# Token halves of the gate matmuls dealt out anew over the attention units of a two-layer hybrid encoder

## The chip, the cores and the metric

The kernel runs on one core of one Trainium2 chip. The metric is the device time of one execution in microseconds, as the median of several runs; lower is better.

## The reference, cut to what matters

Two layers are computed for 512 prompt tokens and 8 streams of 16 tokens each (640 tokens in all, model width 1024). What matters of a layer:

```
z  = x @ w_in                      # q, k, v of mixer A; latents of mixer B
yA = sliding-window attention, prompt (chunks of 64, window 128) and 8 streams (cache of 128)
yB = latent attention,         prompt (512 keys, causal by chunk) and 8 streams (cache of 512)
g  = sigmoid(x @ w_gate + b_gate)  # 1024 -> 2048, needs x alone
h  = g[:, :1024] * (yA @ w_proj_a) + g[:, 1024:] * (yB @ w_proj_b)
x  = LN1(alpha * x + h @ w_out);  x = LN2(alpha * x + ConvGLU(x))
```

The logits x @ w_gate depend on neither mixer, so their matmuls can stand anywhere between the units of attention.

## The kernel before, in words

Everything is written out by hand: each engine has its own program, in a fixed order, and they meet at semaphores. Dense products split both operands into a high and a low part (`x_hi`, `x_lo`, `w_hi`, `w_lo`) and take three matmuls per tile. A slab of weights arrives by a DMA of SP's queue in `w_raw`; ACT writes its high part (`high`, the copy of L791) and POOL its low part (`low`, the subtraction of L704), half a slab at a time.

Attention is a list of 40 units (`UNITS`), u = 0 to 39: u = 0 to 7 are mixer A's prompt ("Ap", 128 queries and four heads each), u = 8 to 15 mixer A's streams ("As", one stream each), u = 16 to 39 mixer B ("Bp", "Bp", "Bs" in turn). PE's loop over u does, in this order: `scores(u + 2)` (L1782 for Ap, L1792 and L1793 for As, L1798 for Bp, L1805 to L1808 for Bs), `turn(u)` (transposes of the probabilities, L1826), the gates behind u, and `values(u - 1)` (L1859, L1862, L1863, L1869). DVE's loop does `peaks(u + 2)` (bias, maximum, negated maximum: L1237 to L1240 for Ap, L1243 to L1246 for As), its half of the copy of the turned probabilities (L1274, not for Ap), `normalise(u + 1)` (L1262, L1263, L1267), which `turn(u + 1)` waits for, and `take_out(u - 1)` (L1285, L1291). ACT's loop does its part of the turned copy (L872, L873), `exps(u + 2)` (L849 for Ap, L853 for As) and `take_gate` (L881).

A gate here is one token half (320 tokens) of one tile of 128 gate columns: 24 matmuls of L1892 into PSUM bank 7, g = 0 to 31 (`NG`). Gates 0 and 1 stand ahead of the loop; `gates_before(u)` says how many stand before unit u, and PE, ACT and SP's order of stores and loads all follow from it. After a gate with odd g, `take_gate` also calls `high` for half a slab of later gate weights (the slab two further on), and POOL's `low` of the same half follows at once. SP's loop over quarters of gates places `load_gate`, `store_gate` and `load_cache` (the cache of a mixer B stream, three DMAs) by the same function.

Of the kernel before, what the change touches and what calls it, by code (L numbers as in the profile page):

```python
# [133 lines left out]
UNITS = [("Ap", i, g) for i in range(NB) for g in range(GH // 2)] + [("As", r, 0) for r in range(NREQ)]  # L134
# [4 lines left out]
NU = len(UNITS)  # L139
# [5 lines left out]


NG = 4 * KD
assert NU % 4 == 0 and NG == 2 + 3 * NU // 4


def gates_before(u):
    return 2 + 3 * (u // 4) + min(u % 4, 3)


def gate_behind(u):

    return range(gates_before(u), gates_before(u + 1))


def quarter_at_scores(u):  # L160
    return 0 if u < 2 else 4 * gates_before(u - 2)
# [2001 lines left out]
```

## Time and profile before

| | |
|---|---|
| median of 3 runs | 1901.82 us (1900.15 to 1901.82) |
| profiled execution | 1900.86 us |
| its span | 1899.1 us |
| PE busy | 1847.1 us, 97% of the span |
| DVE, ACT, POOL busy | 1014.7, 654.4, 541.0 us |

Mixer A takes some 80 us in each layer (layer 0 from 126 us on, layer 1 from 1056 us on). In a timeline a row gives the start, the duration, the engine, the line and the operation, and in brackets how long the engine was idle ahead of it and who ended that. PE's instructions overlap, so a row's duration reaches into the next. "PEclk" is the granted clock as a share of the full one: 1.00 is 2.4 GHz and 0.50 is 1.2 GHz.

### The profile page before, as it was taken

How to read it: one execution, taken by the hardware profiler on the slowest of the kernel's cores; microseconds unless marked ns; L12 is line 12 of the kernel's file. 1: busy time of each engine (PE TensorE's matmuls, PEld its weight loads, DVE VectorE, ACT ScalarE, POOL GpSimd, SP SyncE). 2: the span in 40 equal slices, each digit the busy share in tenths (PEclk: the TensorE clock that was granted, in tenths of full speed). 3: DMA queues.
4: the chain of work that ended last, by engine and by line, in shares of the span. 5: the costliest groups of instructions: out<-in, count | busy, mean ns of one | idle time of the engine just before them, and what ended most of it. 6: DMA issues, size and time to landing. Idle time of an engine off the chain costs nothing. (4 is left out here: it accounts for less than half of the span.)

```text
span 1899.1 us, 31847 instructions
## 1 busy us (share of the span) xinstructions
PE 1847.1 (97%) x12458; PEld 1755.0 (92%) x12458; DVE 1014.7 (53%) x1597; ACT 654.4 (34%) x1381; POOL 541.0 (28%) x244
## 2 busy tenths in 40 slices
PE   8899999999999999999999999999999999999996
PEld 8877888899999999999998788889999999999995
DVE  3567544558854423443765865445697443234447
ACT  4135333532433212332332443334334332132323
POOL 2321211133143234332422311112322333433331
PEclk9999999999999999999999999999999999999998
DMA  6443233232122122121241613323311211222121
GB/s 183 141 140 82 90 110 99 93 129 83 45 92 80 50 89 89 66 72 56 88 135 56 171 47 126 104 69 132 117 68 67 89 55 67 77 89 81 49 74 56
DMA packets 67875, 171.19 MB, mean 90 GB/s; under 512 B 16360, under 2 KB 34456, under 8 KB 60056
## 3 DMA queue, kind: packets, MB, share of 16 engines
q1 hardware_dynamic: 67768, 169.71, 27.6%
q8 instruction: 74, 1.21, 0.3%
q14 instruction: 33, 0.27, 0.1%
HBM read 150.90 MB, written 19.59 MB: 90 GB/s over the span
## 5 line engine op out<-in xcount | busy, mean ns | idle before, releaser
L704 POOL TENSOR_TENSOR w_lo<-w_raw,w_hi 128x1024 fp32r<-128x1024 f32 (+2 forms) x230 | 530.7, 2316 | 1285.8 <-ACT w_hi L791 1266.6
L791 ACT ACTIVATE w_hi<-w_raw 128x1024 fp32r<-128x1024 f32 (+2 forms) x228 | 218.2, 975 | 463.3 <-PE ps L1625 427.1
L1625 PE MATMUL ps<-x_hi,w_hi 128*128 128x320 f32 x1408 | 322.0, 310 | 4.0 <-POOL w_lo L704 4.0
L1625 PE MATMUL ps<-x_lo,w_hi 128*128 128x320 f32 x1408 | 321.3, 309 | 0.0
L1625 PE MATMUL ps<-x_hi,w_lo 128*128 128x320 f32 x1408 | 321.3, 309 | 0.0
L1625 PEld LDWEIGHTS ps<-x_hi,w_hi 128*128 128x128 f32 x1408 | 236.0, 188 | 4.6 <-issue 4.4
L1625 PEld LDWEIGHTS ps<-x_lo,w_hi 128*128 128x128 f32 x1408 | 235.9, 188 | 0.0
L1625 PEld LDWEIGHTS ps<-x_hi,w_lo 128*128 128x128 f32 x1408 | 235.9, 188 | 0.0
L1525 DVE TENSOR_SCALAR f_conv<-f_ext,vec 128x656 f32<-128x656 f32 x44 | 64.6, 1469 | 202.2 <-ACT tail L1016 199.7
L1892 PE MATMUL ps<-x_hi,w_hi 128*128 128x320 f32 x512 | 164.9, 322 | 0.0
L1892 PE MATMUL ps<-x_lo,w_hi 128*128 128x320 f32 x512 | 159.2, 311 | 0.0
L1892 PE MATMUL ps<-x_hi,w_lo 128*128 128x320 f32 x512 | 159.2, 311 | 0.0
L1625 PE MATMUL ps<-hf_hi,w_hi 128*128 128x320 f32 x624 | 143.0, 310 | 0.0
L1625 PE MATMUL ps<-hf_lo,w_hi 128*128 128x320 f32 x624 | 142.5, 309 | 0.0
L1625 PE MATMUL ps<-hf_hi,w_lo 128*128 128x320 f32 x624 | 142.2, 309 | 0.0
L1540 DVE TENSOR_TENSOR hf_lo<-f_h,hf_hi 128x640 f32 x44 | 83.9, 1908 | 46.7 <-ACT hf_hi L1024 46.7
L1625 PEld LDWEIGHTS ps<-hf_hi,w_hi 128*128 128x128 f32 x624 | 104.7, 188 | 0.3
L1625 PEld LDWEIGHTS ps<-hf_lo,w_hi 128*128 128x128 f32 x624 | 104.7, 188 | 0.0
L1625 PEld LDWEIGHTS ps<-hf_hi,w_lo 128*128 128x128 f32 x624 | 104.6, 188 | 0.0
L1892 PEld LDWEIGHTS ps<-x_hi,w_hi 128*128 128x128 f32 x512 | 97.4, 190 | 1.2 <-ACT logits L881 0.3
L1892 PEld LDWEIGHTS ps<-x_lo,w_hi 128*128 128x128 f32 x512 | 97.5, 190 | 0.0
L1892 PEld LDWEIGHTS ps<-x_hi,w_lo 128*128 128x128 f32 x512 | 97.1, 190 | 0.0
(281 smaller groups left out, 3189.5 us busy)
## 6 DMA issues: line engine op xcount, KB each, us to landing
w_raw<-in_slabs SPq DMA_DIRECT2D x84, 1024.0 KB, 4.9
w_raw<-in_slabs SPq DMA_DIRECT2D x20, 768.0 KB, 4.1
gate_logits<-logits SPq DMA_DIRECT2D x64, 160.0 KB, 1.9
gates<-gate_logits SPq DMA_DIRECT2D x16, 640.0 KB, 6.2
w_raw<-in_slabs SPq DMA_DIRECT2D x16, 640.0 KB, 3.7
ckvc<-in_ckvc SPq DMA_DIRECT2D x16, 256.0 KB, 2.7
ckvc_t<-in_ckvc_t SPq DMA_DIRECT2D x16, 256.0 KB, 3.0
w_raw<-in_slabs SPq DMA_DIRECT2D x6, 512.0 KB, 5.9
```

The source lines that it names most:

```text
L704: pool.tensor_tensor(to, w_raw[:, s % 2, c], hi.bitcast(F32), ALU.subtract).then_inc(wlo_ready, 1)
L791: A(w_hi[:, s % 2, c], w_raw[:, s % 2, c], ACT.Copy).then_inc(whi_ready, 1)
L1525: link(TSC(f_conv[:, 0:NC_], f_ext[:, 2:EXT], w(2), vec[:, bass.ds(V_CB + j, 1)], ALU.mult, ALU.add))
L1540: TT(row(hf_lo, jj), f_h[:], row(hf_hi, jj).bitcast(F32), ALU.subtract).then_inc(fh_lo_ready, 1)
L1625: ins = MM(out_[:, a, :], w, x[:, t, a * HT:(a + 1) * HT], start=t == 0 and w is wh and x is hi, stop=t == tiles - 1 and w is wl)
L1892: ins = MM(ps[:, 7, 0:HT], w, x[:, t, a * HT:(a + 1) * HT], start=t == 0 and w is wh and x is x_hi, stop=t == KD - 1 and w is wl)
```

## The change

The number of gates behind each unit was given by a formula, three in every four units, with none behind u = 3, 7, 11, 15 and so on. Now it is a list. Each of the 8 units of mixer A's prompt has one gate, the streams of mixer A have one behind every second unit (u = 8, 10, 12, 14), and mixer B keeps three in four. The total over mixer A is 12 either way, so that two gates move from behind u = 9 and u = 13 to behind u = 3 and u = 7, and from u = 16 on every gate is where it was.

```diff
 NG = 4 * KD
-assert NU % 4 == 0 and NG == 2 + 3 * NU // 4
+HALVES = [1] * 8 + [1, 0] * 4 + [1, 1, 1, 0] * 6
+assert len(HALVES) == NU and [x[0] for x in UNITS[:16]] == ["Ap"] * 8 + ["As"] * 8 and sum(HALVES) == NG - 2
 
 
 def gates_before(u):
-    return 2 + 3 * (u // 4) + min(u % 4, 3)
+    return 2 + sum(HALVES[:u])
```

Every line behind the list stands one line further down in the kernel of the change (L1892 is L1893 there, and so on).

**PE, end of unit u = 2 to the start of u = 4.** The first rows are of before: values of u = 1, scores of 5, turn of 3, values of 2, scores of 6, turn of 4, and the gate of u = 4.

```order
L1859 MATMUL ps<-probs_t,v_tok 64x256 x2
L1782 MATMUL ps<-k_t,q_a 128x256 x4
L1826 MATMUL ps<-ident,probs 128x128 x8
L1859 MATMUL ps<-probs_t,v_tok 64x256 x4
L1782 MATMUL ps<-k_t,q_a 128x256 x4
L1826 MATMUL ps<-ident,probs 128x128 x8
L1892 MATMUL ps<-x_hi,w_hi 128x320
```

The same place on PE in the change:

```order
L1860 MATMUL ps<-probs_t,v_tok 64x256 x2
L1783 MATMUL ps<-k_t,q_a 128x256 x4
L1827 MATMUL ps<-ident,probs 128x128 x8
L1893 MATMUL ps<-x_hi,w_hi 128x320
L1893 MATMUL ps<-x_lo,w_hi 128x320
L1893 MATMUL ps<-x_hi,w_lo 128x320
```

A gate (these three rows eight times over) now stands between the turn of u = 3 and the values of u = 2; the same happens at u = 7.

**ACT, units 12 and 13 of before.** Each unit is the turned copy (L873), the exponentials (L853, L855) and, where there is a gate, L881; L791 is the high part of weights behind an odd gate, here g = 11.

```order
L873 ACTIVATE probs_t<-ps 128x128
L853 ACTIVATE probs,st_sum<-ps,st_nm 128x144
L855 ACTIVATE st_es<-st_d 128x1
L881 ACTIVATE logits<-ps,vec 128x320
L791 ACTIVATE w_hi<-w_raw 128x1024
L873 ACTIVATE probs_t<-ps 128x128
L853 ACTIVATE probs,st_sum<-ps,st_nm 128x144
L855 ACTIVATE st_es<-st_d 128x1
L881 ACTIVATE logits<-ps,vec 128x320
```

In the change the same gate g = 11 stands behind u = 10, and these are units 10, 11 and 12 on ACT:

```order
L874 ACTIVATE probs_t<-ps 128x128
L854 ACTIVATE probs,st_sum<-ps,st_nm 128x144
L856 ACTIVATE st_es<-st_d 128x1
L882 ACTIVATE logits<-ps,vec 128x320
L792 ACTIVATE w_hi<-w_raw 128x1024
L874 ACTIVATE probs_t<-ps 128x128
L854 ACTIVATE probs,st_sum<-ps,st_nm 128x144
L856 ACTIVATE st_es<-st_d 128x1
L874 ACTIVATE probs_t<-ps 128x128
L854 ACTIVATE probs,st_sum<-ps,st_nm 128x144
L856 ACTIVATE st_es<-st_d 128x1
L882 ACTIVATE logits<-ps,vec 128x320
```

Before, the unit behind the conversion of weights had a gate; in the change the unit behind it (u = 11) has none.

## Rows read from the trace of the kernel before

**Rows 1.** The page: busy time by engine; TensorE's granted clock in 40 slices.

```profile
PE 1847.1 (97%) x12458; PEld 1755.0 (92%) x12458; DVE 1014.7 (53%) x1597; ACT 654.4 (34%) x1381; POOL 541.0 (28%) x244
...
PEclk9999999999999999999999999999999999999998
```

**Rows 2.** Lines, PE, 1071 to 1151 us: busy, mean, idle before.

```profile
L1826 PE MATMUL ps<-ident,probs 128*128 128x128 f32 x69 | 10.9, 284 | 3.1 <-DVE probs L1267 3.1
```

**Rows 3.** PE's timeline behind u=3 and u=7 (layer 1): start, duration, row, idle.

```profile
1092.68 1.09 PE L1826 MATMUL ps<-ident,probs 128*128 128x128 f32 x8 [1.35 <-DVE probs L1267]
...
1114.80 0.44 PE L1826 MATMUL ps<-ident,probs 128*128 128x128 f32 x2 [0.92 <-DVE probs L1267]
```

**Rows 4.** PE's timeline around u=11, layer 1.

```profile
1129.65 0.44 PE L1792 MATMUL ps<-kc_t,q_a 64*64 64x128 f32 x4
...
1130.09 0.44 PE L1826 MATMUL ps<-ident,probs 128*128 128x128 f32 x2
...
1131.16 0.44 PE L1792 MATMUL ps<-kc_t,q_a 64*64 64x128 f32 x4
1131.43 0.25 PE L1793 MATMUL ps<-k_t,q_a 64*64 64x16 f32 x4
1132.14 0.44 PE L1826 MATMUL ps<-ident,probs 128*128 128x128 f32 x2 [0.46 <-DVE probs L1267]
```

**Rows 5.** PE's timeline behind the gate of u=12, layer 1.

```profile
1136.93 0.25 PE L1793 MATMUL ps<-k_t,q_a 64*64 64x16 f32 x4
1137.10 0.44 PE L1826 MATMUL ps<-ident,probs 128*128 128x128 f32 x2
```

**Rows 6.** POOL's timeline: the low parts behind the gates of u=6 and u=12.

```profile
1111.58 2.36 POOL L704 TENSOR_TENSOR w_lo<-w_raw,w_hi 128x1024 fp32r<-128x1024 f32 x1 [9.93 <-ACT w_hi L791]
...
1137.74 2.41 POOL L704 TENSOR_TENSOR w_lo<-w_raw,w_hi 128x1024 fp32r<-128x1024 f32 x1 [9.57 <-ACT w_hi L791]
```

**Rows 7.** DVE's timeline behind the gates of u=6 and u=12.

```profile
1112.14 1.81 DVE L1245 SCALAR_TENSOR_TENSOR st_nm<-st_mx,nsink_s 128x1 f32<-128x1 f32 x1
...
1137.94 2.22 DVE L1245 SCALAR_TENSOR_TENSOR st_nm<-st_mx,nsink_s 128x1 f32<-128x1 f32 x1
...
1140.86 0.30 DVE L1267 TENSOR_SCALAR probs<-probs,st_ri 128x144 f32<-128x144 f32 x1
```

**Rows 8.** PE's timeline at u=15: scores of u=17, turn of 15.

```profile
1146.65 0.71 PE L1798 MATMUL ps<-kb,qb 100*128 100x128 f32 x4
1147.19 0.38 PE L1826 MATMUL ps<-ident,probs 128*128 128x128 f32 x2
```

**Rows 9.** DVE's timeline: the normalising of u=6.

```profile
1102.64 1.14 DVE L1267 TENSOR_SCALAR probs<-probs,st_ri 128x256 f32<-128x256 f32 x4
```

**Rows 10.** PE's timeline: the turn of u=6.

```profile
1105.31 1.09 PE L1826 MATMUL ps<-ident,probs 128*128 128x128 f32 x8
```

**Rows 11.** Stretches: us, PE, PEld, DVE, ACT, POOL, PEclk, DMA, GB/s.

```profile
1087.00:1093.50 6.50, 5.15 (x41) 3.53 (x40) 5.47 (x13) 3.94 (x15) 0.00 (x0) 1.00 0.46 166
...
1147.80:1151.20 3.40, 3.07 (x14) 1.85 (x13) 3.32 (x8) 0.90 (x5) 2.27 (x1) 1.00 0.09 34
1151.20:1154.60 3.40, 3.40 (x15) 3.40 (x14) 1.66 (x7) 1.07 (x3) 0.00 (x0) 0.50 0.00 0
```

**Rows 12.** PE's timeline, around the gate of u=16, both layers.

```profile
220.30 0.44 PE L1826 MATMUL ps<-ident,probs 128*128 128x128 f32 x2 [0.33 <-DVE probs L1267]
...
224.09 0.39 PE L1862 MATMUL ps<-probs_t,vc 128*128 128x128 f32 x2
...
1150.92 0.51 PE L1826 MATMUL ps<-ident,probs 128*128 128x128 f32 x2 [0.33 <-DVE probs L1267]
...
1156.26 0.38 PE L1862 MATMUL ps<-probs_t,vc 128*128 128x128 f32 x2
```

**Rows 13.** SP's timeline: the last DMA of stream 0's cache.

```profile
1141.71 0.63 SPq L623 DMA_DIRECT2D krc_t<-in_krc_t  x1
```

**Rows 14.** The tile ckvc_t in layer 1: DMA issue to landing.

```profile
DMA to landing us min/median/max: 2.6/3.0/6.1
```

## The prediction

> **What bounds the kernel now.** The page comes first: PE is busy for 1847.1 of 1899.1 us, no other engine for much over half the span, and its granted clock stands at 9 tenths or more in nearly every slice [rows 1]. The time is therefore PE's own work plus the moments in which it waits. The change keeps every matmul, so only those moments can move, and only in mixer A. The view by lines, for mixer A of layer 1, puts all of them before the turn of a unit's probabilities: 3.1 us, all released by DVE's normalising, L1267 [rows 2]. PE's timeline then shows the places, and each lies behind a unit without a gate: 1.35 us before turn(4), behind u = 3, and 0.92 us before turn(8), behind u = 7 [rows 3]; 0.46 us before turn(12), behind u = 11 [rows 4]; and 0.33 us before turn(16), behind u = 15 [rows 12]. Layer 0 has the same four waits in the same sizes, the last of them among the rows.
>
> Why they are there follows from the order of the two programs. DVE does peaks(u + 2) before normalise(u + 1), so that turn(u + 1) waits until DVE has worked through the scores that PE issued just ahead of turn(u). A gate gives PE 24 matmuls, and 3.5 us, to do in the meantime. With a gate the margin is comfortable even in the prompt: the last normalising of u = 6 ends at 1102.64 + 1.14 = 1103.78 us [rows 9], and PE begins that turn only at 1105.31 us [rows 10], 1.53 us later.
>
> **What the change removes.** A gate behind u = 3 and behind u = 7 covers both waits, 1.35 + 0.92 = 2.27 us a layer. The units now look like u = 5 and 6 of before, and I take the cover for complete: 3.5 us of gate against 1.35 us. Behind g = 7 and g = 9 POOL's low part of weights now falls among DVE's peaks of stream units that PE follows with a gate; it costs up to 2.3 us of DVE (next part) and is hidden by those 3.5 us. Were that cover gone, each would cost PE about what the wait before turn(8) costs now, 0.92 us.
>
> **What it adds.** The units 9, 11, 13 and 15 have no gate now, 11 and 15 alone had none before. I price each from rows of this kernel with the same neighbours.
>
> (1) u = 9 follows a gate with even g, without a conversion of weights, as u = 11 does before: 0.46 us [rows 4].
>
> (2) u = 11 follows g = 11, an odd gate. Behind it ACT converts half a slab and POOL subtracts, for 2.41 us from 1137.74 us on in the trace [rows 6]. In just these 2.41 us a DVE instruction on a single column, L1245, which starts 0.20 us after POOL's, takes 2.22 us and ends with it. The same instruction took 1.81 us behind the gate of u = 6, where it started at 1112.14 us and POOL's ran from 1111.58 for 2.36 us [rows 6, 7]: in both places it ends 0.01 to 0.02 us after POOL's. So DVE stands until POOL has finished. Before, u = 13 with its gate stood behind this place. In the change nothing does. DVE's chain gives the time of the turn: the normalising ends at 1140.86 + 0.30 = 1141.16, and a turn starts 0.06 us behind it, at 1141.22 (estimate, the 0.06 from the next rows: hence also the choice not to round). PE gets there earlier. Its turn starts at 1137.10 [rows 5]; from a turn to the next scores without a gate between is 1131.16 - 1130.09 = 1.07 us, and those scores end 1131.43 + 0.25 - 1131.16 = 0.52 us after their start [rows 4]. That is 1137.10 + 1.07 + 0.52 = 1138.69, and the wait is 1141.22 - 1138.69 = 2.53 us. The bounds are 0.46 us (POOL disturbs nothing) and 2.53 us; I take 2.53, since the row it comes from has the same instructions in the same order up to the missing gate.
>
> (3) u = 13 follows an even gate, but PE now has the longer scores of u = 16 to do. From scores(13) to turn(12) is 1132.14 - 1129.65 = 2.49 us through DVE [rows 4]. PE needs 1130.09 - 1129.65 = 0.44 us to its turn, 1.07 us to the scores and 0.71 us for them [rows 8], 2.22 us in all. The wait is 0.27 us.
>
> (4) u = 15 follows g = 13 before and after: 0.33 us, unchanged.
>
> **Loads and stores.** Gates 5 to 11 come one or two units earlier, the loads of gate slabs with them. Stream 0's cache is asked for at the end of scores(15) either way, and scores(18) now follow it by one gate and not two. After scores(15) PE has 0.44 + 1.07 + 0.27 + 0.71 us to turn(14), a gate unit of 5.0 us and about 1 us more, some 8 us in all. The cache's last DMA takes 0.63 us to issue [rows 13], and the loads of that tile land in 2.6 to 6.1 us, the longest being the one that before stood behind a slab [rows 14]. That slab now comes two units earlier. I cost this at nothing; without the cover the worst landing would still be in time by about half a microsecond.
>
> **The sum of the waits.** Per layer 1.35 + 0.92 + 0.46 = 2.73 us go, and 0.46 + 2.53 + 0.27 = 3.26 us come: 0.53 us more, 1.06 us over both layers.
>
> **The clock.** One thing beside the waits moves with them. In layer 1 the stretch 1147.8 to 1151.2, with small matmuls, no gate and 0.33 us idle, is followed by 3.4 us at 0.50, which is 1.2 GHz; the stretch around u = 3, with 1.35 us idle but the fuller matmuls of the prompt, keeps 1.00 (2.4 GHz) [rows 11]. The slow stretch costs what the gate of u = 16 shows in the two layers: 1156.26 - 1150.92 = 5.34 us against 224.09 - 220.30 = 3.79 us, 1.55 us [rows 12]. Layer 0 has the same instructions at full clock, so it is partly luck where it strikes. The new place behind g = 11 has 2.53 us idle and the smallest matmuls of the kernel around it, with less work than the place that lost the clock. A slow stretch there costs between 0 and 1.55 us a layer. I count one of two, 1.55 us.
>
> TensorE: Matmul & The Clock Gate, in the table of why this matters for a kernel, in the Trainium skill, warns only of idle gaps longer than any computed here. By this rule the sum would be 1.06 us alone; the row at 1151.2 us, slow behind 0.33 us of idle time, speaks against it.
>
> **Sum.** 1900.86 + 1.06 + 1.55 = 1903.47 us for the profiled execution. The median shown lies 1901.82 - 1900.86 = 0.96 us above it, so the forecast is 1904.4 us.
>
> **Rivals.** (a) The clock stays up at the new wait: 1900.86 + 1.06 + 0.96 = 1902.9 us. For it: three of the four waits of each layer leave the clock alone. Chance 0.20. (b) It falls in both layers: 1903.47 + 1.55 + 0.96 = 1906.0 us, slower by 0.22%. For it: the light work around the gap. Chance 0.25. (c) The gain side: DVE does not stand behind POOL at u = 11, since a small shift lets L1245 start ahead of POOL's instruction (0.20 us decide it). Then the wait there is 0.46 us, the layers gain 2.73 - 1.19 = 1.54 us each, and the time is 1901.82 - 3.08 = 1898.7 us; if the slow stretch behind u = 15 also goes, 1897.2 us, the one case that ends faster by more than 0.2%. Against it: the instructions behind L1245 on DVE touch the same memory, and one of them would stand instead. Chance 0.13. (d) The change does nothing that can be seen, because PE was never short at u = 3 and 7: against it stand both waits in both layers; it has no chance of its own. (e) Something waits that nothing here shows, ACT for a stored gate or PE for the cache, at some microseconds: 1906 us or more, chance 0.07. What is left for one slow stretch, the forecast, is 0.35.
>
> **How the numbers follow.** About 0.2% (3.8 us) is what a measurement of this kernel can tell from no change. The limits are 1898.0 and 1905.6 us. Faster takes part of (c), 0.05. Slower takes (b) a little over its edge, part of (e), 0.28. The rest, 0.67, is no change that can be told. The range runs from (c), 1898.7, to a little over (b), 1906.6; the forecast's own range, with 0.5 us of spread to either side, is 1903.9 to 1904.9.
>
> **What would show it.** In the profile after, PE waits for nothing before turn(4) and turn(8); it waits 0.46 us before turn(10), 2.5 us before turn(12), 0.3 us before turn(14) and 0.33 us before turn(16), each for L1268, in both layers. In the wait before turn(12) DVE's L1246 lasts 2.2 us beside POOL's L705. The gate of u = 12 takes 3.8 us, or about 5.3 us where the clock fell. I am wrong if turn(12) starts without a long wait, if turn(4) or turn(8) still wait, or if the time moves by more than 5 us, which no row here could explain.

## The result and the profile after

The change makes the kernel slower. The median is 1907.02 us (1905.5 to 1908.4, 8 runs) against 1900.92 us (1899.82 to 1901.82, 8 runs), a difference of 6.1 us. The ratio is 1.0032, with a 95% interval of 1.0021 to 1.0043, so that the difference is clear of the measurement's uncertainty though small. The forecast was 1904.4 us with a range up to 1906.6; the time lies 0.4 us above the range. Three executions that appear further down lay far above the rest of their kernel (2021.01 and 6737.64 us of the kernel before, 3023.85 us of the run with the filled pause) and are left out of every median.

The page of the kernel after the change, busy time and granted clock, for [rows 1]:

```profile
PE 1853.5 (97%) x12458; PEld 1760.7 (92%) x12458; DVE 1017.8 (53%) x1597; ACT 654.2 (34%) x1381; POOL 541.2 (28%) x244
...
PEclk9999999999999999999999999999999999999998
```

The page alone shows no cause. PE does the same 12458 matmuls and is busy for 6.4 us more, 1853.5 against 1847.1 us. More busy time for the same work means slower matmuls, so that the clock has to be looked at, not only the waits.

The view by lines, PE, mixer A of layer 1, for [rows 2]; the last column is the idle time before these instructions and who ended it:

```profile
L1827 PE MATMUL ps<-ident,probs 128*128 128x128 f32 x70 | 11.4, 289 | 3.5 <-DVE probs L1268 3.5
```

PE waits 3.5 us there against 3.1 us. PE's timeline in layer 0 after the change shows the turns one by one. The rows are turn(4), (8), (10), (12), (13), (14) and (16), for [rows 3, 4, 12]:

```profile
158.75 1.09 PE L1827 MATMUL ps<-ident,probs 128*128 128x128 f32 x8
...
189.99 0.44 PE L1827 MATMUL ps<-ident,probs 128*128 128x128 f32 x2
...
197.36 0.44 PE L1827 MATMUL ps<-ident,probs 128*128 128x128 f32 x2 [0.46 <-DVE probs L1268]
...
206.37 0.69 PE L1827 MATMUL ps<-ident,probs 128*128 128x128 f32 x2 [2.45 <-DVE probs L1268]
...
213.93 0.44 PE L1827 MATMUL ps<-ident,probs 128*128 128x128 f32 x2
...
215.98 0.44 PE L1827 MATMUL ps<-ident,probs 128*128 128x128 f32 x2 [0.27 <-DVE probs L1268]
...
224.78 0.44 PE L1827 MATMUL ps<-ident,probs 128*128 128x128 f32 x2 [0.33 <-DVE probs L1268]
```

The waits before turn(4) and turn(8), 1.35 and 0.92 us before, are gone. Those before turn(10), turn(12) and turn(14) are 0.46, 2.45 and 0.27 us, and turn(16) keeps its 0.33 us. Behind u = 11 this is what DVE and POOL do, for [rows 6, 7]:

```profile
203.18 2.15 DVE L1246 SCALAR_TENSOR_TENSOR st_nm<-st_mx,nsink_s 128x1 f32<-128x1 f32 x1
...
206.02 0.29 DVE L1268 TENSOR_SCALAR probs<-probs,st_ri 128x144 f32<-128x144 f32 x1
```

```profile
202.97 2.34 POOL L705 TENSOR_TENSOR w_lo<-w_raw,w_hi 128x1024 fp32r<-128x1024 f32 x1 [10.31 <-ACT w_hi L792]
```

DVE's instruction on one column per partition takes 2.15 us instead of 0.16, and ends with POOL's subtraction, at 205.33 and 205.31 us. The normalising ends at 206.31 and turn(12) starts at 206.37 us.

The stretches behind the long wait in layer 0 and in layer 1, and the one of the gate of u = 16 in layer 1, for [rows 11]. The columns are the stretch, its length, busy time of PE, PEld, DVE, ACT and POOL with their instructions, the granted clock, and the DMA's share and rate:

```profile
206.40:212.90 6.50, 6.50 (x28) 6.42 (x28) 1.93 (x10) 0.84 (x4) 0.00 (x0) 0.56 0.47 161
...
1141.60:1148.30 6.70, 6.70 (x29) 6.50 (x29) 1.90 (x9) 0.92 (x5) 0.00 (x0) 0.57 0.49 157
...
1160.20:1163.60 3.40, 3.40 (x25) 3.40 (x24) 1.73 (x7) 1.07 (x3) 0.00 (x0) 1.00 0.02 5
```

The gate of u = 12, which follows the long wait, runs at a clock of 0.56 and 0.57, hence nearly all of it at 1.2 GHz, in both layers. From turn(12) to turn(13) PE takes 213.93 - 206.37 = 7.56 us, where a unit of the same kind took 4.96 us before [rows 4, 5]: 2.6 us lost. The gate of u = 16 in layer 1, slow in the trace of before, runs at full clock here: from turn(16) to turn(17) PE takes 5.07 us, and took 6.61 us before.

One more difference stands ahead of the first gate that moved, where both kernels do the same. This is the second part of the slow stretch at the start of mixer A in layer 0, first of before, then of the change:

```profile
140.60:144.00 3.40, 3.40 (x25) 3.40 (x24) 3.23 (x8) 1.32 (x6) 2.41 (x1) 0.97 1.14 293
```

```profile
140.60:144.00 3.40, 3.40 (x15) 3.40 (x14) 3.23 (x8) 1.36 (x6) 2.36 (x1) 0.52 1.20 266
```

Both traces fall to 1.2 GHz near the end of a wait of 3.4 us there, but for 3.4 us before and for 6.8 us in this execution of the change, in both layers. From the start of mixer A to turn(2) it takes 28.75 and 28.82 us where before took 27.53 and 27.59, 2.45 us in all. The other eight profiles have the long stretch there in 2 of 16 layers, so it is not a mark of the change. The profiled execution is the slowest of the eight (1908.4 us). Its 7.5 us above the profile of before are therefore, in us: waits 0.9, the gate of u = 12 5.2, the start of mixer A 2.45, the gate of u = 16 in layer 1 -1.5, and 0.5 left over.

### The profile page after: what moved, and what is told of

The parts are those of the page before. It is cut to its first block and busy times, and to the rows that moved or that the text cites. A ratio compares the mean times of both kernels' runs of the same rounds, so it can differ in the third digit from the quotient of the medians.

```text
span 1906.6 us, 31847 instructions
## 1 busy us (share of the span) xinstructions
PE 1853.5 (97%) x12458; PEld 1760.7 (92%) x12458; DVE 1017.8 (53%) x1597; ACT 654.2 (34%) x1381; POOL 541.2 (28%) x244
## 5 line engine op out<-in xcount | busy, mean ns | idle before, releaser
L1893 PE MATMUL ps<-x_hi,w_hi 128*128 128x320 f32 x512 | 167.3, 327 | 0.0
L1893 PE MATMUL ps<-x_lo,w_hi 128*128 128x320 f32 x512 | 161.6, 316 | 0.0
L1893 PE MATMUL ps<-x_hi,w_lo 128*128 128x320 f32 x512 | 161.4, 315 | 0.0
L1893 PEld LDWEIGHTS ps<-x_hi,w_hi 128*128 128x128 f32 x512 | 99.7, 195 | 1.1 <-ACT logits L882 0.3
L1893 PEld LDWEIGHTS ps<-x_lo,w_hi 128*128 128x128 f32 x512 | 99.6, 194 | 0.0
L1893 PEld LDWEIGHTS ps<-x_hi,w_lo 128*128 128x128 f32 x512 | 99.2, 194 | 0.0
```

Source lines behind the costliest of these rows:

```text
L1893: ins = MM(ps[:, 7, 0:HT], w, x[:, t, a * HT:(a + 1) * HT], start=t == 0 and w is wh and x is x_hi, stop=t == KD - 1 and w is wl)
```

## The experiments

Three theories stood against each other. **A**: POOL's low part of weights, which follows an odd gate, holds DVE; with no gate behind it PE waits some 2.45 us, and the thin stretch around that wait takes the clock down. **B**: the clock falls because the stream units have fewer gates, whatever DVE does. **C**: the slow stretches are chance and have nothing to do with the change. A median of before, 1900.93 us, stands beside the first four runs, and 1901.32 us beside the last three. Differences from the change are taken from its 1907.02 us, which was measured apart from these; measured once more beside the last three runs, the change took 1906.37 us, so each such difference is uncertain by some 0.6 us.

### POOL's subtraction moved under a gate

The kernel of the change, with one wait more on POOL:

```diff
+                    if late is not None and half == 1:
+                        pool.wait_ge(turned, late)
...
+                    if s == S_GATE + 4:
+                        low(s, s, layer, late=(layer * NU + 12 + 1))
```

> The kernel of the change, with one wait more on POOL: its low part of the half slab behind g = 11 starts only when turn(12) is done, and so lies under the gate of u = 12. Theory A (POOL's subtraction holds DVE, PE waits 2.45 us behind u = 11, and that pause takes TensorE's clock down for 6.8 us): the wait before turn(12) is 0.46 us, the gate of u = 12 takes 3.8 us, and the time is 1907.0 - 2 x 2.0 - 2 x 2.6 = 1897.8 us. Theory B (the clock falls because the stream units now have a gate only behind every second unit, whatever DVE does): only the waits go, 1903.0 us. Theory C (the clock's slow stretches are chance and do not belong to the change): 1903.0 us too, but with slow stretches in other places.

Measured: 1897.92 us (1897.49 to 1898.86), ratio to before 0.9983 (0.9974 to 0.9992), 9.1 us below the change. PE before turn(12), POOL's subtraction, DVE's instruction that stood before, and the stretch of the gate behind turn(12):

```profile
203.98 0.44 PE L1831 MATMUL ps<-ident,probs 128*128 128x128 f32 x2 [0.46 <-DVE probs L1272]
```

```profile
204.57 2.40 POOL L707 TENSOR_TENSOR w_lo<-w_raw,w_hi 128x1024 fp32r<-128x1024 f32 x1 [12.31 <-PE ps L1831]
```

```profile
202.78 0.16 DVE L1250 SCALAR_TENSOR_TENSOR st_nm<-st_mx,nsink_s 128x1 f32<-128x1 f32 x1
```

```profile
204.00:207.60 3.60, 3.60 (x25) 3.58 (x26) 3.42 (x9) 0.66 (x4) 2.40 (x1) 1.00 0.00 0
```

DVE's instruction takes 0.16 us again, the wait is 0.46 us, and the gate behind it runs at full clock. The places of all gates are still those of the change. So the placement alone, with no wait above 0.46 us, takes no clock here (against B as stated), and neither cost is chance (against C): 9.1 us go with one wait on POOL. The traces divide them. From turn(2) to turn(16) this run takes 67.6 us in each layer and the profile of the change 72.2 and 72.3 us, 9.2 us more; 2 x (2.45 - 0.46) = 4.0 us of it is waiting, and the unit of the gate of u = 12 takes 4.98 us in place of 7.56 and 7.61 us, which is the clock's 5.2 us. How much the clock costs in another execution of the change varies (the last run below).

### The pause filled with matmuls

```diff
+                    if u == 11:
+                        pe.wait_ge(gate_taken, layer * NG + gates_before(u) + 1)
+                        for k in range(12):
+                            MM(ps[:, 7, 0:HT], w_hi[:, 0, 0:P], x_hi[:, k % KD, 0:HT], start=True, stop=True)
```

> The kernel of the change, with 12 extra matmuls of 320 columns on PE between turn(11) and values(10), whose result is overwritten and used by nobody (1.8 us of work, no part of the reference). DVE is still held by POOL. Theory A: the end of the pause is DVE's and doesn't move, so the 1.8 us of filling cost nothing; idle time before turn(12) is about 0.7 us, the clock stays up, and the time is 1907.0 - 5.2 = 1901.8 us. Theory B and C: the clock falls as before, 1907 us. If PE's order rather than DVE set the end, it would be 1907.0 + 3.6 = 1910.6 us.

Measured: 1903.4 us (1902.42 to 1904.48), ratio 1.0012 (1.0002 to 1.0022), 3.6 us below the change. PE's filling (L1918) and turn(12), and the stretch of the gate behind it:

```profile
202.47 2.01 PE L1918 MATMUL ps<-x_hi,w_hi 128*128 128x320 f32 x12
...
206.36 0.44 PE L1827 MATMUL ps<-ident,probs 128*128 128x128 f32 x2 [0.80 <-DVE probs L1268]
```

```profile
206.50:210.10 3.60, 3.60 (x26) 3.58 (x26) 1.84 (x9) 0.84 (x4) 0.00 (x0) 1.00 0.91 286
```

From turn(11) to turn(12) it is 4.06 us, against 4.04 us with 12 matmuls less, since DVE sets the end; the wait shrinks to 0.80 us, and the clock stays at 1.00, in layer 1 too. PE does more work, and the kernel is faster than the change. This shows the clock's part without touching DVE or POOL. The gain is 3.6 us and not the expected 5.2. From turn(2) to turn(16) the trace takes 69.7 us in each layer, 5.1 us less in both together than the profile of the change, but 3.9 us less than the profile of the change once more, where one slow stretch was shorter. Part of the rest shows up outside mixer A: from turn(16) of layer 0 to the scores of u = 2 in layer 1 this run takes 848.81 us, and the run before it 848.07 us. Why the filling costs 0.7 us there was not followed up.

### Only even gates ahead of the units without one

```diff
-HALVES = [1] * 8 + [1, 0] * 4 + [1, 1, 1, 0] * 6
+HALVES = [1] * 7 + [0] + [1, 1, 0, 1, 1, 0, 1, 0] + [1, 1, 1, 0] * 6
```

> Gates behind u = 0 to 6, 8, 9, 11, 12 and 14: twelve again, and each of the units 7, 10 and 13 without one follows a gate with even g, which converts no weights (u = 15 as before). Theory A: waits behind u = 7 none (DVE has 2.0 us of work where PE has 2.5), behind u = 10 0.46, u = 13 0.27 and u = 15 0.33 us, 1.06 us against 3.06 us before in each layer, no slow clock: 1900.9 - 4.0 = 1896.9 us. Theory B (gates taken from the streams cost the clock): one or two slow stretches a layer, 1900 to 1902 us. Theory C: between these, by chance.

Measured: 1896.84 us (1895.9 to 1897.45), ratio 0.9975 (0.9964 to 0.9986), the expected time within 0.1 us. PE's timeline at turn(8), turn(11) and turn(14):

```profile
186.94 0.44 PE L1827 MATMUL ps<-ident,probs 128*128 128x128 f32 x2
...
199.30 0.44 PE L1827 MATMUL ps<-ident,probs 128*128 128x128 f32 x2 [0.46 <-DVE probs L1268]
...
211.28 0.44 PE L1827 MATMUL ps<-ident,probs 128*128 128x128 f32 x2 [0.26 <-DVE probs L1268]
```

Turn(8) follows a unit without a gate and yet waits for nothing: the gate ahead of that unit has an even g, POOL does nothing from 181.4 to 192.5 us, and DVE's one-column instruction takes 0.16 us, where it took 1.81 us at this place before [rows 7]. So the wait of 0.92 us before turn(8) in the kernel before was POOL's work too. The two others wait 0.46 and 0.26 us, and no gate behind turn(3) runs slow in either layer. Nothing in DVE's program differs from before.

### The long wait alone, in the kernel before

```diff
-HALVES = [1] * 8 + [1, 0] * 4 + [1, 1, 1, 0] * 6
+HALVES = [1, 1, 1, 0] * 2 + [1, 1, 0, 1, 1, 1, 1, 0] + [1, 1, 1, 0] * 6
```

> The kernel before with one gate's place changed: none behind u = 10, one behind u = 11. The prompt keeps its pauses behind u = 3 and u = 7, and the unit without a gate now follows the odd gate g = 9. The number of gates among the streams is that of before. Theory A: the wait there is 2.45 us and not 0.46, and the clock falls: 1900.9 + 2 x 2.0 + 2 x 2.6 = 1910.1 us. Theory B (too few gates among the streams): their number is unchanged, so the waits alone, 1904.9 us. Theory C: 1904.9 us give or take a slow stretch.

Measured: 1908.45 us (1905.97 to 1909.74), ratio 1.0035 (1.0023 to 1.0048), 7.5 us above before. Turn(11), which follows the unit without a gate, in layer 0, and the stretches behind it in layers 0 and 1:

```profile
199.48 0.44 PE L1827 MATMUL ps<-ident,probs 128*128 128x128 f32 x2 [2.45 <-DVE probs L1268]
```

```profile
199.70:203.70 4.00, 4.00 (x19) 4.00 (x18) 1.76 (x9) 0.84 (x4) 0.00 (x0) 0.58 0.00 0
1134.20:1140.00 5.80, 5.80 (x27) 5.80 (x26) 1.63 (x8) 0.84 (x4) 0.00 (x0) 0.59 0.00 0
```

The wait is the expected 2.45 us in a kernel that has as many gates among the streams as before, and the clock falls behind it in both layers. Waits of 2 x 2.0 us leave 3.5 us for the clock, where 5.2 were expected: in layer 0 the slow stretch lasts 3.4 us here, in layer 1 6.8 us, and the units with the slow gate lose 1.5 and 2.3 us. B as a matter of the number of gates, with 1904.9 us, falls.

### Two units without a gate, one behind the other

```diff
-HALVES = [1] * 8 + [1, 0] * 4 + [1, 1, 1, 0] * 6
+HALVES = [1] * 8 + [1, 0, 1, 1, 0, 0, 1, 0] + [1, 1, 1, 0] * 6
```

> The prompt as in the change (a gate behind each of u = 0 to 7), the stream gates behind u = 8, 10, 11 and 14: the odd gate g = 11 is followed by a unit with a gate, and u = 12 and 13 have none, one behind the other. Number of gates among the streams as in the change. Theory A: no long pause; 0.46 us behind u = 9 and u = 12, about 0.9 us behind u = 13, where DVE needs about 2.5 us a unit and PE 1.5, and 0.33 us behind u = 15, 2.15 us against 3.5 us in the change, no slow clock from them: 1907.0 - 2.7 - 5.1 = 1899.2 us. Theory B (too few gates among the streams take the clock down): 1904.3 us.

Measured: 1902.55 us (1900.64 to 1903.87), ratio 1.0006 (0.9997 to 1.0015): no difference from before that can be told, and 3.4 us above the 1899.2 expected. Turn(13), and the stretches around it and of the gate of u = 14 in layer 0, then of the same gate in layer 1:

```profile
209.15 0.44 PE L1827 MATMUL ps<-ident,probs 128*128 128x128 f32 x2 [0.46 <-DVE probs L1268]
```

```profile
206.20:209.10 2.90, 2.49 (x26) 1.87 (x24) 2.12 (x11) 1.36 (x5) 0.00 (x0) 1.00 0.91 249
209.20:211.70 2.50, 2.46 (x12) 1.59 (x13) 2.26 (x12) 0.84 (x4) 0.00 (x0) 0.81 1.00 369
211.70:214.00 2.30, 2.30 (x10) 2.30 (x9) 1.31 (x6) 1.09 (x5) 0.00 (x0) 0.50 0.14 52
...
1142.70:1146.00 3.30, 3.30 (x14) 3.30 (x14) 1.31 (x6) 1.08 (x5) 0.00 (x0) 0.50 0.10 38
```

The longest pause in the streams is 0.46 us, and still the gate of u = 14, the next after these units, runs at 0.50, 1.2 GHz, in both layers; in layer 0 the clock fell before it began (0.81 over the 2.5 us ahead of it). Over the 2.9 us shown first PE was busy for 2.49 us. The two slow gates lose 1.2 and 1.55 us, and in layer 1 the gate of u = 16 is slow as well (1.55 us). So theory A was too narrow in its second half, and the measured time lies between its 1899.2 us and the 1904.3 us of B. It takes no long pause to lose the clock: from the last gate to the next PE has 5.5 to 5.6 us here, and 5.2 to 5.4 us in the change, with only the small matmuls of stream units, by its timeline. With the subtraction moved under a gate that stretch is 3.2 us long, and the clock stays. Length alone doesn't decide it either: the stretch ahead of the gate of u = 16 is 5.0 to 5.1 us with 0.33 us of waiting and lost the clock in 2 of 16 layers (before and this run, layer 1), the one ahead of the gate of u = 8 in the kernel before and in the run with the long wait alone 5.1 us with 0.92 us and never did. What decides between them was not tested. On the other point too the expectation missed: 0.9 us of waiting behind u = 13 was expected, and there are 0.27 us or less.

### The best placement, with the last stall moved too

The placement of the even gates, and the half behind g = 13 held back in the same way as in the first experiment (`S_GATE + 5`, half 0, until turn(16)).

> The placement of the run with only even gates ahead of the units without one (none behind u = 7, 10, 13, 15), and also POOL's low part behind g = 13 held back until turn(16) is done, so that it lies under the gate of u = 16. Theory A: the wait of 0.33 us before turn(16) goes in both layers, and the other waits stay at 0.46 and 0.27 us: 1896.84 - 0.66 = 1896.2 us. Rival: the subtraction, moved by 3 us, stands in DVE's way behind u = 16 or the load of a gate slab that waits for it comes late, and PE waits there instead: 1896.8 us or more.

Measured: 1895.80 us (1894.98 to 1896.41), ratio 0.9971 (0.9959 to 0.9982). PE at turn(16), POOL's subtraction and the DVE instruction beside it:

```profile
218.28 0.44 PE L1831 MATMUL ps<-ident,probs 128*128 128x128 f32 x2
```

```profile
218.87 2.40 POOL L707 TENSOR_TENSOR w_lo<-w_raw,w_hi 128x1024 fp32r<-128x1024 f32 x1 [12.95 <-PE ps L1831]
```

```profile
219.60 1.95 DVE L1272 TENSOR_SCALAR probs<-probs,st_ri 128x128 f32<-128x128 f32 x2
```

The wait of 0.33 us is gone. The median is 1.0 us below that of the even gates, where 0.66 were expected; the ranges of the two overlap, so that the time alone doesn't show the gain, and the trace does. DVE still stands behind POOL (1.95 us for two small instructions), but now under a gate, where nobody waits. This is the fastest version of the study, 11.2 us below the change (10.6 below its second median) and 5.5 us below the kernel before beside it.

### The change once more

> The kernel of the change, unchanged, once more. Theory A: 1907 us, waits of 2.45 us before turn(12), and a slow clock behind it in both layers; whether it lasts 3.4 or 6.8 us each time is what the run is to show. Theory C (slow stretches are chance): in at least one layer none behind turn(12).

Measured: 1906.37 us (1905.78 to 1908.98), ratio 1.0031 (1.0021 to 1.0041). The stretches behind turn(12) in layer 0 (two rows) and in layer 1:

```profile
205.70:209.10 3.40, 3.40 (x16) 3.38 (x15) 1.83 (x9) 0.84 (x4) 0.00 (x0) 0.56 0.91 299
209.20:213.00 3.80, 3.80 (x30) 3.33 (x28) 1.17 (x5) 0.81 (x2) 0.00 (x0) 0.96 0.11 40
...
1139.40:1145.70 6.30, 6.30 (x28) 6.22 (x28) 1.90 (x9) 0.84 (x4) 0.00 (x0) 0.57 0.50 166
```

The clock fell behind turn(12) in both layers again. In layer 0 it came back after 3.4 us, in layer 1 it was low through the whole gate. The fall belongs to the change; its length varies from one execution to the next. The units with the slow gate take 6.51 and 7.42 us, so that they lose 1.5 and 2.5 us.

## Why the prediction was wrong

**The waits were right, and so was the direction.** The most likely outcome was put as no change that can be told (0.67), slower had 0.28; the time rose by 6.1 us where 2.6 were forecast, and more than the 5 us that the prediction itself named as a sign of being wrong. The long wait before turn(12) was forecast at 2.53 us and is 2.45 us; the others are 0.46, 0.27 and 0.33 us as forecast. Turn(4) and turn(8) wait for nothing. The mechanism, a one-column instruction of DVE that stands until POOL's subtraction ends, is shown by the run that moved the subtraction. The sum of the waits was forecast at +1.06 us and is 2 x (3.51 - 3.06) = +0.9 us. Loads and stores of gates cost nothing, and stream 0's cache was in time: no turn or scores waits for them.

**The step that failed is the clock.** "I count one of two, 1.55 us": the fall was right in place, but mis-sized twice over. It comes in both layers, in the two profiles of the change and in the one with the long wait alone, six times of six, so that one of two was too few. And it mostly lasts longer than the one stretch that the prediction took its price from: the gate behind it loses 2.3 to 2.6 us in four of these six, and 1.5 us in two. For both layers of the change that is 4.0 us in one profile and 5.2 in the other, against 1.55. With the 0.9 us of waits and the 0.5 us left over, what belongs to the change adds up to 5.4 to 6.6 us; the medians differ by 6.1 us.

**The base of the sum was the second error, and a smaller one.** The 1900.86 us already hold the slow gate of u = 16 in layer 1, 1.55 us by the prediction's own pricing, which stands in 2 of the 16 layers traced with that wait and in neither profile of the change. The sum keeps it in the forecast, and only rival (c) lets it go. The 0.96 us from the profile to the median came from three executions; over the eight of before it is 0.06 us. Both terms put the forecast too high, so that the clock was mis-sized by more than the 2.6 us between forecast and result. In rival (a), "three of the four waits of each layer leave the clock alone" is true of layer 1; in layer 0 all four do.

**The upper bound was wrong too.** Rival (b), the fall in both layers, was priced at 1906.0 us with the 1.55 us of a single row. The fall in both layers is what happened, and it had a chance of 0.25. "A slow stretch there costs between 0 and 1.55 us a layer" took one slow stretch of 3.4 us as the worst case. The trace of before had a longer one elsewhere, 6.8 us at 1.2 GHz during and behind a wait of 3.95 us, which could have warned:

```profile
65.40:72.20 6.80, 3.18 (x12) 3.21 (x13) 5.38 (x6) 3.19 (x4) 4.67 (x2) 0.52 0.83 247
```

**The rule of the page failed as it was said.** The section on why this matters for a kernel in the Trainium skill, TensorE: Matmul & The Clock Gate, warns of idle gaps longer than the 2.45 us here, and by it the clock would have stayed up. The trace shows it falling behind 2.45 us in the change, and behind 0.46 us at most in the run with two units without a gate, one behind the other. In both cases PE had only the small matmuls of stream units around its gaps.

**The rivals.** (a), the clock stays up, did not happen in either profile of the change. (c), L1245 ahead of POOL, did not happen; in every profile with that neighbourhood DVE stood. (e) found nothing.

The gain of the change was real and was given back. Its two prompt gates save 2.27 us a layer. The placement of the even gates saves the same, with a gate behind u = 3 and none needed behind u = 7, adds no long wait, since of its units without a gate only u = 15 follows an odd one, and takes 1896.84 us.

## What to carry to other kernels

Where an engine's filler work is dealt over waits, look at what the filler brings with it on the other engines: here every second gate sends a 2.4 us subtraction to POOL, and DVE stands for it. The units without filler belong behind those that bring nothing, or the subtraction belongs under the next filler, which one semaphore wait does. Price a stretch in which PE has only small matmuls by the clock too, and look through the whole trace for the longest slow stretch, not only at the nearest; a few useless matmuls in that stretch made the kernel faster than the change, though not faster than the kernel before. Before a profiled difference is put to a change, look whether the clock differs where both kernels do the same.

## What the runs showed that was not expected

The clock fell in or behind 5.5 to 5.6 us of small matmuls with no wait longer than 0.46 us, with PE nearly always busy by the profile. And the length of a slow stretch behind the same instructions is 3.4 us in one layer and 6.8 us in the other of one execution (the run with the long wait alone, and the change once more), and at the start of mixer A it is 3.4 us in 14 of 18 layers and 6.8 us in 4. This may be why the change's runs spread from 1905.5 to 1909.0 us; that was not tested.
